# Queries and keys of neighbourhood pairs two to five as 2x2 block products in an encoder trunk on one core

## The reference

```python
def na_layer(a, mem_k, mem_v, w_in, w_out, rpb):
    proj = a @ w_in
    q, k, v, mq = jnp.split(proj, [TOK_WIDTH, 2 * TOK_WIDTH, 3 * TOK_WIDTH], axis=-1)
    o = neighbourhood_attention(to_heads(q, 12), to_heads(k, 12), to_heads(v, 12), rpb)
    m = memory_attention(mq, mem_k, mem_v)
    return jnp.concatenate([from_heads(o), m], axis=-1) @ w_out
```

## Time and profile before

| | |
|---|---|
| median of 3 runs | 2205.66 us (2205.24 to 2205.95) |
| the profiled execution | 2205.68 us, span 2203.9 us, mean granted clock of TensorE 0.998 |
| PE busy | 2187.2 us, 99% of the span |
| DVE, ACT, POOL busy | 1295.4, 924.2, 1179.5 us |
| memory phase, pair phase | about 1164 to 1264 us and 1264 to 1490 us of the span |

### The profile page before, as it was taken

How to read it: one execution, slowest core, us unless ns; L and a number is a source line. 1 busy time by engine, 2 the same in 40 slices (tenths; PEclk the granted TensorE clock), 3 DMA queues, 4 the chain that set the end, 5 groups by cost and what they waited for, 6 DMA issues and landing times.

```text
span 2203.9 us, 31940 instructions
## 1 busy us (share of the span) xinstructions
PE 2187.2 (99%) x11542; PEld 1797.4 (82%) x11542; DVE 1295.4 (59%) x2161; ACT 924.2 (42%) x1851; POOL 1179.5 (54%) x951
## 2 busy tenths in 40 slices
PE   9999999999999999999999999999999999999998
PEld 8778888888888888888889877778878888888887
DVE  7896666657544444676853255554675434447767
ACT  6633233365233232344663355464723233234454
POOL 1276655678988888200334433416798878870001
PEclk9999999999999999999999999999999999999999
DMA  8011112553343333743453533335433433348334
GB/s 334 30 39 48 63 53 87 172 189 97 135 161 102 101 108 98 285 158 97 130 161 106 151 74 74 82 125 186 148 105 122 147 115 101 100 129 316 97 99 163
DMA packets 130970, 280.37 MB, mean 127 GB/s; under 512 B 31983, under 2 KB 46590, under 8 KB 128766
## 3 DMA queue, kind: packets, MB, share of 16 engines
q1 hardware_dynamic: 130814, 278.33, 38.8%
HBM read 207.76 MB, written 70.54 MB: 126 GB/s over the span
## 4 chain that ended last, share of the span: by engine, by line
PE 93%; POOL 3%; ACT 1%; DVE 1%; issue 1%; DMA 0%; SPq 0%; DVEq 0%; POOLq 0%; ACTq 0%
PE PS L2724 28%; PE PS L2726 28%; PE PS L2725 27%; PE PS L2999 2%; POOL OPS L1116 2%; PE PS L3265 2%; PE PS L3247 1%; PE PS L3165 1%; PE PS L2986 1%; PE PS L3032 1%; POOL TW L1140 1%; PE PS L3152 1%; PE PS L3176 0%; PE PS L3178 0%; PE PS L3180 0%
## 5 line engine op out<-in xcount | busy, mean ns | idle before, releaser
L2724 PE MATMUL PS<-AOP,OPS 128*128 128x512 f32 x1216 | 474.4, 390 | 1.1 <-POOL OPS L1116 0.6
L2726 PE MATMUL PS<-AOP,OPS 128*128 128x512 f32 x1216 | 473.2, 389 | 0.0
L2725 PE MATMUL PS<-AOP,OPS 128*128 128x512 f32 x1216 | 473.2, 389 | 0.0
L1116 POOL TENSOR_TENSOR OPS<-TW,OPS 128x512 fp32r<-128x512 f32 x174 | 263.0, 1526 | 78.6 <-ACT OPS L1487 77.3
L1050 POOL TENSOR_TENSOR wlo<-stage,whi 128x512 fp32r<-128x512 f32 (+1 forms) x120 | 153.8, 1304 | 236.4 <-ACT whi L1380 236.2
L2724 PEld LDWEIGHTS PS<-AOP,OPS 128*128 128x128 f32 x1216 | 228.2, 188 | 51.4 <-POOL OPS L1116 2.4
L2726 PEld LDWEIGHTS PS<-AOP,OPS 128*128 128x128 f32 x1216 | 228.2, 188 | 47.4
L2725 PEld LDWEIGHTS PS<-AOP,OPS 128*128 128x128 f32 x1216 | 228.3, 188 | 47.1
L1487 ACT ACTIVATE OPS<-TW 128x512 fp32r<-128x512 f32 x176 | 106.6, 628 | 344.0 <-POOL TW L1140 321.7
L2724 PE MATMUL PS<-OPS 128*128 128x512 f32 x584 | 227.7, 390 | 0.3
L2726 PE MATMUL PS<-OPS 128*128 128x512 f32 x584 | 227.2, 389 | 0.0
(11 more groups left out here) (334 smaller groups left out, 4695.4 us busy)
## 6 DMA issues: line engine op xcount, KB each, us to landing
stage<-in_w SPq DMA_DIRECT2D x100, 512.0 KB, 3.8
hidden_scratch<-HT SPq DMA_DIRECT2D x154, 256.0 KB, 2.2
SRAW<-hidden_scratch SPq DMA_DIRECT2D x154, 256.0 KB, 2.7
stage<-in_wpack SPq DMA_DIRECT2D x76, 512.0 KB, 3.8
BW<-in_w SPq DMA_DIRECT2D x16, 1024.0 KB, 8.2
h_scratch<-Hb SPq DMA_DIRECT2D x24, 512.0 KB, 3.8
Hb<-h_scratch SPq DMA_DIRECT2D x24, 512.0 KB, 6.0
cat_scratch<-OC SPq DMA_DIRECT2D x14, 512.0 KB, 2.9
```

The source lines that it names most:

```text
L1116: pool.tensor_tensor(place[:, 1, :], w1_operand(l, j, p), place[:, 0, :].bitcast(F32), ALU.subtract)\
L2724: pe.matmul(dst, stat[0], mov[0], start=start, stop=False, skip_group_check=onto)
L2725: pe.matmul(dst, stat[0], mov[1], start=False, stop=False, skip_group_check=onto)
L2726: return pe.matmul(dst, stat[1], mov[0], start=False, stop=stop, skip_group_check=onto)
```

## The change

For pairs two to five (units U_NAH + 4 to U_NAH + 11) the product of weights and tokens is a product of 2x2 blocks: the four token blocks are the two halves of the tokens times the two halves of the 1024 inputs, and the four weight blocks are queries and keys times the two halves of the inputs. Seven block products with sums of blocks replace eight. A block product is four triples, so a pair takes 28 triples where it took 32. What this adds:

- nine steps of token sums on POOL (`token_step`, four instructions of 128x512 each), once, from which ACT makes 16 high parts (`token_hi`) and DVE 16 low parts (`token_lo`);
- for each of the four pairs: four weight sums and seven low parts on POOL (`pair_sum`, `pair_lo`), seven high parts and a copy on ACT (`pair_hi`, `pair_one`), five adds on DVE (`pair_add`); the split of whole units (`his`, `los`) and the key copy fall away;
- another order of the loads on SP.

```diff
+NA_ORDER = "1726543"
...
+            los(U_V + 12)
+            pool.wait_ge(pre_sq, 26)
+            pool.wait_ge(a_lo, a_before(7))
+            token_step(0, one, part(1, 0, 0), part(1, 1, 0), ALU.add)
+            token_step(1, diff, one, part(0, 0, 0), ALU.subtract)
+            token_step(2, diff, diff, part(0, 1, 0), ALU.subtract)
+            los(U_NAH + 3)
+            token_step(3, one, one, part(1, 0, 4), ALU.add)
+            token_step(4, one, one, part(1, 1, 4), ALU.add)
             los(U_NAH + 4)
-            for hp in range(HP):
-                if hp + 1 < HP:
-                    mask_bias(hp + 1)
-                los(min(U_NAH + 2 * hp + 6, U_OUT1 + 2))
+            pool.wait_ge(pv, R_ROW)
+            token_step(5, two, diff, part(1, 0, 4), ALU.add)
+            token_step(6, two, two, part(1, 1, 4), ALU.add)
+            mask_bias(1)
+            pool.wait_ge(*USED[U_NAH + 2])
+            token_step(7, four, part(0, 0, 4), two, ALU.subtract)
+            token_step(8, four, four, part(0, 1, 4), ALU.add)
+            for i in range(HP - 2):
+                pair_sum(i, "7")
+                pair_lo(7 * i)
+                pair_lo(7 * i + 1)
+                for p in "564":
+                    pair_sum(i, p)
+                pair_lo(7 * i + 2)
+                if i + 2 < HP:
+                    mask_bias(i + 2, (0, 1))
+                pair_lo(7 * i + 3)
+                pair_lo(7 * i + 4)
+                if i + 2 < HP:
+                    mask_bias(i + 2, (2, 3))
+                pair_lo(7 * i + 5)
+                pair_lo(7 * i + 6)
...
+            HI_AT = {11: 0, 14: 1, 15: 2, 2: 3, 4: 4, 6: 5, 9: 6}
...
+                if 1 <= T < 5:
+                    token_hi("7", T - 1)
+                if 7 <= T < 11:
+                    token_hi("6", T - 7)
+                if 15 <= T < 19:
+                    token_hi("5", T - 15)
+                if 19 <= T < 23:
+                    token_hi("3", T - 19)
...
+            def token_lo(p, k):
+                hi, lo = na_tokens(p, 0, k), na_tokens(p, 1, k)
+                dve.wait_ge(*token_done(t_hi, p, k))
+                if p in "76":
+                    dve.wait_ge(t_sum, TS0 + (28 if p == "7" else 32))
+                dve.tensor_tensor(lo, raw_sum(p, k), hi.bitcast(F32), ALU.subtract).then_inc(t_lo, 1)
...
+            LO_STEPS = {"7": (8, 9, 10, 11), "6": (14, 15, 16, 17), "5": (18, 19, 20, 21), "3": (22, 23, 25, 27)}
+            ADDS_AT = {8: ("u2", "u3"), 10: ("22",), 12: ("21",), 14: ("12",)}
...
-        LO_AT = (-3, 0, 2, 4, 8, 10, 14, 16)
+        LO_AT = (-2, 0, 2, 4, 8, 10, 14, 16)
...
                 piece, t = T + 1, T - (HP - 1) * ROWS
-                if piece < (HP - 1) * ROWS:
+                if piece < ROWS:
                     project(U_NAH + 2 + piece // KD, piece % KD)
+                elif piece < (HP - 1) * ROWS:
+                    i, at_p = divmod(piece - ROWS, ROWS)
+                    for m in range(28 * at_p // ROWS, 28 * (at_p + 1) // ROWS):
+                        pair_product(7 * i + m // 4, m % 4)
```

More of the change, by code:

```diff
@@ L67 @@
 N_RET = 14 * (RH - 1)
+NA_BLOCKS = range(U_NAH + 4, U_OUT1)
+NA_ORDER = "1726543"
+NA_BANK = {"1": 0, "2": 0, "6": 1, "7": 2, "4": 2, "5": 3, "3": 3}
+NA_SUMS = "7564"
+NA_ADDS = ("u2", "u3", "22", "21", "12")
+N_NA = 7 * (HP - 2)
 def unit_rows():
@@ L307, in trunk_program @@
             taken_by(U_NA + n, "a")
-        for n in range(2 * HP):
-            taken_by(U_NAH + n, "ad"[n % 2 and n < 2 * HP - 1])
+        for n in range(4):
+            taken_by(U_NAH + n, "ad"[n % 2])
         def tiles_before(t):
@@ L1022, in _ @@
                     load_values(hp + 1)
+                    load_units(U_NAH + 2 * hp + 6)
             load_units(U_OUT1 + 5)
```

245 lines of the change are left out of this document (219 added, 26 removed).

## The result

The changed kernel takes 2209.37 us (median of 20 runs, 2207.66 to 2211.20), the kernel before 2205.49 us on the same chips (20 runs, 2204.01 to 2206.78). The ratio is 1.0017, with an interval of 1.0011 to 1.0024: slower, by 2.4 to 5.3 us. The forecast was 2204.3, with a range of 2199.0 to 2211.0. So the time lies in the range, while the sign is the wrong one: nine tenths of the saving were to be given back, and all of it and a third more were. The profiled execution took 2208.59 us, its span is 2206.8 us.

The account below looks back on a forecast made before the run. PE's own work, busy for 99% of the span, was taken as the bound. The terms, -11.2 + 4.2 + 1.7 + 3.5 + 0.4 = -1.4 us against 2205.7, gave 2204.3 us, range 2199.0 to 2211.0.

Parts of the forecast that it names:

- Term 1: Pairs two to five: four triples fewer in each of four pairs, 16 x 0.70 us, saving 11.2 us.
- Terms 2 and 3: Ahead of pair one: PE waits 4.2 us for U_NAH's low part behind token sums; slower clock afterwards costs 1.7 us.
- Term 4: Pair one, steps 14 to 23: DVE's work exceeds PE's time; PE waits 3.5 us at odd rows' transposes.
- Rival 3: Pair one: POOL is the bound, instructions taking 1.74 us; PE waits 4 to 5 us at products; about 2207; chance 0.11.
- Term 5, "later pairs: zero": Pairs after the first: POOL, DVE and ACT all have room for the added work, so nothing is lost.
- the sign at 35.5 us: Later pairs: a pair taking more than 35.5 us would break the forecast upwards; 34.6 us was expected.
- Rival 2: Pairs two to five: POOL contention makes DVE late 0.3 us a turn, adding 9.6 us, 2213.9; chance 0.16.
- Term 5, the end: Output phase: the first output block's low part moves one step later on DVE, costing at most 0.4 us.

Follow-up runs that it names:

- e13_bias_between: e12_best with the second half of each pair's bias split too, the sixth product's low part between its quarters on POOL; 2196.32 us, ratio 0.9955.
- e1_units_first: The changed kernel with POOL's low parts of U_NAH + 3 moved ahead of the token sums; 2211.51 us, ratio 1.0028.
- e2_lows_early: The changed kernel with DVE's four low parts of the third token sum moved from steps 14 to 17 to steps 12, 13, 16, 17; 2211.64 us.
- e12_best: e9_even_one_port with three order edits: first product's low part earlier, first bias half split around the fourth's, and the edit of e11_low_first; 2199.80 us.
- e9_even_one_port: e7_units_one_port with each pair's four one-product steps on even steps, as in e4_even_singles; 2201.12 us, ratio 0.9978.
- e14_two_element: e13_bias_between with the pair phase's row normalisation back in its first form, without the edit of e6_one_port; 2206.58 us, ratio 1.0003.
- e11_low_first: e10_dve_sums with DVE's low part of the second output phase's first piece moved ahead of the last sum of keys; 2205.84 us, ratio 0.9998.
- e6_one_port: The changed kernel with DVE's pair-phase row normalisation as a multiplication with an added 0 and an accumulator output; 2207.51 us, ratio 1.0008.
- e7_units_one_port: The changed kernel with both the order of e1_units_first and the normalisation form of e6_one_port; 2201.31 us, ratio 0.9980.
- e5_linked: e1_units_first with every POOL token-sum instruction waiting for the end of the one before it, leaving short gaps; 2207.69 us, ratio 1.0008.
- e10_dve_sums: e9_even_one_port with eight of POOL's token sums made by DVE and POOL's second-pair bias ahead of token step 5; 2206.78 us, ratio 1.0001.
- e3_bias_later: The changed kernel with POOL's low part for each pair's fourth product moved ahead of the first half of the next bias; 2215.16 us, ratio 1.0042.
- e4_even_singles: The changed kernel with each pair's four one-product steps moved from odd steps to even ones; 2209.25 us, ratio 1.0017.

## Why the prediction was wrong

**Term 1, what is removed: right.** 16 x 0.70 us; e13_bias_between gets 9.5 us of the 9.8 due from step 24 to 78.

**Terms 2 and 3, U_NAH late and the clock: right.** 4.2 + 1.7 forecast; 4.07 of wait and 5.6 in all measured, and e1_units_first, which takes only this away, starts step 0 at +0.0 (to be read with the scatter of such starts). The row's 1.26 us for a token sum held (5.05 for four); the rule's two times DVE would have given 1.36, and the wait 1.2 us longer.

**Term 4, DVE in steps 14 to 23: the size was off, and half of the mechanism.** It had 3.5 us at the transposes of odd rows; between steps 10 and 24 4.8 us are lost, 1.2 us of it at scores, since `pair_scores` waits for the peak of the step before, and 1.4 us at POOL's low part. At the transposes of odd rows the longest wait is 0.4 us, and it is for ACT's copy; none is for DVE's normalisation. The term took DVE for the engine that is over its time, at 1.15 us for a low part. The price was right: the eight low parts from 1305 us on took 0.68 (five) or 1.76 us (three), 1.09 on average. But e2_lows_early took DVE's work out of the two steps and lost time, and e12_best, with the same low parts on DVE in steps 10 to 24 and POOL's low parts earlier, loses only 1.0 us there. So some 3.8 us of the 4.8 went with POOL's order, the other DVE form and the moved short steps together; the runs don't part them. That the 3.5 us of the forecast stand near 4.8 is in good part luck. Rival 3 (POOL the bound in the first pair) was nearer the truth, but by order, not because its instructions slow to 1.74 us.

**Term 5, "later pairs: zero": the step that failed.** It was argued from shares: by its terms 24.8 us of POOL and 22.1 of DVE in 34.6. The busy times came nearly as said, 24.0 and 23.2, but waits come from the place of an instruction in its queue, and 2.7 us of 9.1 were lost between steps 24 and 78. Two causes were found: ACT's copy of the even row's transposes, for which the transposes of the odd row wait when the filler between is short (0.2 us, twice a pair), and a low part of POOL that stands behind six instructions of bias, once the first is mended (0.4 us a pair, e9_even_one_port). With both mended a pair takes 35.69 us. In the changed kernel the two waits are 0.4 of the 0.8 us that a pair takes above 35.6; the other 0.4 lies in differences of about 0.1 us and less a step, to which no cause is assigned. The forecast's 34.6 us for a pair was an error of reading besides: the earlier trace rows begins 0.65 us behind the scores of step 16 and ends 0.38 ahead of those of step 32, and from scores to scores pair one took 38.4 us like the later ones. So a pair without any loss takes 35.6, and the sign at 35.5 us would have been passed by that alone. Rival 2 had the losses and the place, not the cause, and three times the size (0.3 us a turn, where 2.7 us over 27 turns are 0.1): contention of DVE with POOL is real (26 us of stretching over the 96 rows), and in the pairs from step 32 on it costs nothing, as e14_two_element shows.

**Term 5, the end: 0.4 forecast, 1.6 measured.** 1.0 us of it is a wait for DVE's low part that stood behind the last sum of keys; e11_low_first takes 0.6 off such a wait. The rest, 0.6 us, goes with a low part of the output phase that lasts 1.78 us beside POOL (0.68 alone): e14_two_element has it too and loses 0.6 us more there than e13_bias_between, and in e6_one_port it lasts 0.69 and 0.6 us less is lost, but it wasn't tried by itself.

Put together: the spans came 4.3 us above the forecast's -1.4. Term 5 is short by 2.7 us in the pairs and 1.2 at the end, term 4 by 1.3; terms 2 and 3 were 0.3 too high, and 0.6 came back in the tail. Without what term 5 left out the spans would differ by -1.0 us, with the sign that was forecast.

The terms asked how much work each engine has; they lacked the question of what stands ahead of the one instruction that PE needs. With the places in the queues mended, and the normalisation in a form that POOL doesn't hold up, 9.3 us of the 11.2 are there by the medians.

**Open.** Why DVE is held for one of POOL's instructions at some times and for six to eight at others. In the changed kernel itself the first normalisation (0.70 us) got in between the third and fourth of eight sums end to end; in e1_units_first the same instructions, with the row 1.5 us earlier against the sums, gave 9.10. With another form on DVE (e7_units_one_port) it isn't there, nor with gaps on POOL (e5_linked), where the two also met at another time; what decides it isn't shown. And most of the 2.7 us between starts of step 0 of like kernels stays unexplained.

## What to carry to other kernels

Where PE is busy for 99%, ask of each new instruction on another engine what stands ahead of it in its queue when PE wants its result, not what share of the time that engine is free: most losses here were of that kind. Cutting a block of seven microseconds in two, with a low part between, took away a wait of 2.41 us and the slow clock behind it (e13_bias_between), while ten microseconds less work for POOL left one of 2.50 us (e10_dve_sums). When one such wait is mended, look at the next block, which PE now reaches earlier, and before an instruction is moved ahead, look whether its own input is there: in e3_bias_later it wasn't, and the engine stood idle for it. And an edit that brings GpSimd's back-to-back work beside VectorE's normalisations can cost nine microseconds at one instruction, so look for the longest single instruction of each kind before you believe a comparison of two orders.

## What was not expected of the hardware

- One VectorE instruction lasted 9.10 us (0.32 alone) while GpSimd ran eight instructions end to end, and ended at the first gap between two of them; the same in e14_two_element (9.09 us). Another lasted 6.88 us (0.68 alone) beside six, and ended when GpSimd had nothing left to do. Beside instructions 0.08 us apart no row of these phases was stretched by more than 1.2 us.
- The same multiplication with an added 0 and an accumulator output takes 0.41 us for 192 elements and 0.58 for 352 (0.32 and 0.40 in the first form), and in none of the eight kernels that had it did one of the 96 last more than 0.01 us longer than the shortest of its width.
- TensorE's clock fell behind waits of 2.41 us (1.00, then 0.50 and 0.65 in e12_best) and 4.07 us, and stayed at 1.00 in the stretches behind waits of 1.42 us (changed kernel) and 1.88 us (e9_even_one_port). The length of the wait alone doesn't decide it: behind 2.31 us in e4_even_singles it fell to 0.50, behind 2.50 us in e10_dve_sums and 2.48 in e11_low_first it stayed at 1.00.
